# Two convolution projections recast as turns of seven products, with one weight sum of 32 turns made by accumulating transfers

## The chip, the cores and the metric

One core of one Trainium2 chip runs the kernel. The metric is the device time of one execution in microseconds (us); lower is better. The kernel before took 1972.85 us, the median of 3 runs (1972.36 to 1973.45).

## What is computed

One layer on x of 512 tokens by 2048 channels, in float32: a gated short convolution and a squared-ReLU MLP, each behind an RMS norm and with a residual sum. With d = 2048 and an MLP width of 8192 it is, cut to what matters:

```
h = rmsnorm(x, mix_norm)
b_gate, c_gate, v = jnp.split(h @ w_in, 3, axis=-1)      # w_in 2048 x 6144
u = c_gate * v
y = depthwise causal convolution of u over 3 tokens      # conv_w 3 x 2048
x = x + (b_gate * y) @ w_out                             # w_out 2048 x 2048
a = relu(rmsnorm(x, mlp_norm) @ w1)                      # w1 2048 x 8192
x = x + (a * a) @ w2                                     # w2 8192 x 2048
```

## The kernel before, in words

Every product of float32 numbers is made of three matmuls on rounded halves: an operand is split into hi, its rounding to the matmul's format (ScalarE), and lo, the rest (VectorE: operand minus hi), and hi·lo, lo·hi and hi·hi are summed in PSUM.

**Stage one, the convolution** (16 blocks): both projections are made directly. A block is 512 output channels; for each of 16 k-tiles of 128 input channels `products` (L992, matmuls at L989) makes 4 x 3 = 12 matmuls of 128x128 by 128x512, 3072 in all. Weights come in 1 MB loads (L262) into two slots of `w_raw`; `split_hi` (L377, ScalarE) and `split_lo` (L599, VectorE) fill a ring of four. Twelve blocks make c, v and b of four groups of channels; VectorE multiplies and convolves them (`take_c`, `take_v`, `take_b`), the four last blocks are the output projection, whose results are added to x in `resid` (`take_resid`, L666), turned to tokens by 64 transposes of 128x128 (`turn`, L1055) and put to DRAM as `mixed`. The sums of squares for the two norms are made by one matmul (L1012) and eight small ones (L1143).

**Stage two, the MLP** (32 turns): the two products are made by a seven-product (Strassen-Winograd) scheme. A turn `v` takes four quadrants of a weight block (R11, R12, R22, R21, 1 MB each, loaded at L265) and makes the products L11, S1, S2, L12, S3, S4, L22 in this order. Each product has 2 slots, so a turn has 14; a slot is 12 matmuls (L1084), a turn 168. VectorE makes the four weight sums T1 to T4 in place in `raw` (`form_weights`, L793), two instructions of 128x1024 each; T3 is used by S3, slots 8 and 9. Each slot's weights are split by `split_turn_hi` (L454, ScalarE) and `split_turn_lo` (L799, VectorE) into a ring of four, so that the split of slot s waits until TensorE is through with slot s-4. Turns 0 to 15 are the first MLP product ("up"), two turns (a pair) for one group of 1024 hidden channels; 16 to 31 are the second ("down").

In an up pair TensorE waits for two turns' products; ScalarE copies them out of PSUM (L475, L483), VectorE adds them up in 12 steps (`add_up`, L824), ScalarE rectifies, TensorE turns them by 32 transposes (`turn_quad`, L1097, in four groups ahead of slots 0, 2, 4 and 5 of the next pair), ScalarE squares, and the seven activation sums are formed (L679), split (L509, L739) and spilled to DRAM by GpSimd's queue (L351, 14 transfers of 512 KB a pair) to be loaded in the down turns. The activations of the up turns are 7 tiles for either turn of a pair; S2, S4 and L22 have one place for both turns and are reloaded every turn from `act_kept` by the SP queue.

Every engine runs one list of instructions in an order written out by hand: a loop over turns and slots, with tables such as `SPLIT_AT` that say at which slot of which turn a step is made. SP's queue issues the loads in order, each behind a wait; GpSimd's queue issues the stores.

The core of a slot on TensorE:

```
pe.wait_ge(lo_ready, SLOTS * v + s + 1)
for k in (2 * half, 2 * half + 1):
    for t in range(2):
        mm = turn_tile(v, j, k, t)
mm.then_inc(used, 1)
```

Of the kernel before, what the change touches and what calls it, by code (L numbers as in the profile page):

```python
# [12 lines left out]
KT = 16  # L13
# [3 lines left out]
GRAN = 4  # L17
NG = KT // GRAN
NRAW = 2
HALF = 256  # L20
ZBUF = 3

SQUARES_AT = {2: (0,), 3: (1,), 4: (2,), 5: (3, 4), 6: (5,), 7: (6, 7), 8: (8, 9),
              9: (10, 11), 10: (12, 13), 11: (14, 15)}
TAKE_AT = (4, 7, 10, 13)
TURN_AT = (8, 10, 12, 14)

OUT_ORDER = (0, 2, 1, 3)
# [9 lines left out]
NPROD = 7  # L38
R11, R12, R22, R21 = range(4)
RAW_OF = (R11, R11, R11, R21, R12, R22, R21)  # L40
# [4 lines left out]
SHARED = (S2, S4, L22)  # L45
# [4 lines left out]
FIRST_SPLIT = {(1, 11): 0, (1, 12): 1, (1, 13): 2, (1, 15): 3, (2, 0): 4, (2, 2): 5, (2, 4): 6}  # L50
FIRST_FORM = {(1, 14): (0, 1), (2, 1): (2,), (2, 3): (3,)}

SECOND = (L11, L12, S1, S3, S2, S4, L22)
SECOND_SPLIT = {(0, 6): 0, (0, 7): 1, (0, 9): 2, (0, 10): 3, (0, 11): 4, (1, 1): 5, (1, 3): 6}
SECOND_FORM = {(0, 8): (0, 1), (0, 10): (2,), (0, 12): (3,)}
# [4 lines left out]
STAGES = 5  # L60
# [4 lines left out]
def conv_mlp_layer(nc, xt, weights, mlp, cols_dram, out, FF):  # L65
# [4 lines left out]
    OUT0 = 3 * NQ  # L70
    NB = OUT0 + NQ
    NC = FF // (2 * BW)
    NP = NQ // 2
    UP = 2 * NC
    NV = UP + NC * NP
    USED = KT * NB
    assert S == BW and DT == KT and NQ == 4 and weights.shape[0] == NG * NB
    assert mlp.shape[0] == 4 * NV and FF // D * 2 == NC

    xt_v = xt.rearrange("(k p) t -> p k t", p=P)  # L80
    out_v = out.rearrange("(j p) f -> p j f", p=P)
    spill = nc.dram_tensor("spill", (NC, NPROD, 2, P, NT, HALF), F32).ap()
    act_kept = nc.dram_tensor("act_kept", (2, NPROD, 2, P, NT, HALF), F32).ap()
# [5 lines left out]
    RESID, H_HI, H_LO, Z_HI, Z_LO, RAW, RING_AT, U_PAD = (base + KB * a for a in (0, 32, 64, 96, 128, 160, 176, 192))  # L89
    TMP = U_PAD + NT * (CW - 1 + S) * 4  # L90
    RSTD = TMP + 4 * KB
    ONES = RSTD + 2 * KB
    EYE = ONES + 512
    COLS = EYE + 512
    NORM = COLS + (2 + CW) * DT * 4

    with ExitStack() as ctx:
# [3 lines left out]
        def sem(name):  # L101
            return ctx.enter_context(nc.semaphore(name))

        resid = at("resid", RESID, [P, DT, S])
        h_hi = at("h_hi", H_HI, [P, DT, S], F32R)
        h_lo = at("h_lo", H_LO, [P, DT, S], F32R)
        z_hi = at("z_hi", Z_HI, [P, KT, S], F32R)
        z_lo = at("z_lo", Z_LO, [P, KT, S], F32R)
        w_raw = at("w_raw", RAW, [P, NRAW, GRAN, BW])
        w_hi = at("w_hi", RING_AT, [P, RING, BW], F32R)  # L110
        w_lo = at("w_lo", RING_AT + 8 * KB, [P, RING, BW], F32R)
        u_pad = at("u_pad", U_PAD, [P, NT, CW - 1 + S])
        tmp = at("tmp", TMP, [P, 2, S])
        rstd_b = at("rstd_b", RSTD, [P, S])
        ones = at("ones", ONES, [P, P])
        eye = at("eye", EYE, [P, P])
        cols = at("cols", COLS, [P, (2 + CW) * DT])
        square, square_sum = tmp[:, 0, :], tmp[:, 1, :]
        var, root = tmp[:, 0, :], tmp[:, 1, :]


        quads1 = at("quads1", H_LO + 24 * KB, [P, 2, NT, HALF])
        quads2 = at("quads2", U_PAD, [P, 2, NT, HALF])
        quad = {"L11": quads1[:, 0], "L21": quads1[:, 1], "L12": quads2[:, 0], "L22": quads2[:, 1]}
        q_s1, q_s2, q_s3, q_s4 = (at(f"sum{n}", RESID + 4 * KB * n, [P, 2, BW]) for n in range(4))

        q_first = at("sum_first", U_PAD, [P, 2, BW])
        q_l22 = at("sum_l22", H_LO + 28 * KB, [P, 2, BW])
        second_s1 = at("second_s1", RESID + 16 * KB, [P, NT, HALF])
        turned_out = [at("turned0", RSTD, [P, BW])] + [at(f"turned{i + 1}", RESID + a * KB, [P, BW])  # L130
                                                        for i, a in enumerate((12, 14, 20, 22))]
        stage = [at(f"stage{i}", a, [P, NT, HALF], F32R)
                 for i, a in enumerate([RESID + (16 + 4 * i) * KB for i in range(4)] + [TMP])]
        acts1 = [at(f"act{j}", H_HI + 8 * KB * j, [P, 2, NT, HALF], F32R) for j in range(NPROD)]
        acts2 = {j: at(f"act2_{j}", Z_LO + 8 * KB * n, [P, 2, NT, HALF], F32R) for n, j in enumerate((L11, S1, L12, S3))}
        raw = at("raw", Z_HI, [P, 4, NT, BW])
        ring = [at("ring0", RAW, [P, 2, 2, BW], F32R), at("ring1", RAW + 8 * KB, [P, 2, 2, BW], F32R),
                at("ring2", RING_AT, [P, 2, 2, BW], F32R), at("ring3", RING_AT + 8 * KB, [P, 2, 2, BW], F32R)]
        var_t, root_t, rstd_t = (at(f"{n}_t", NORM + 32 * i, [P, NT]) for i, n in enumerate(("var", "root", "rstd")))

        x11, x21, x22, x12 = (at(f"x{q}", Z_LO + 8 * KB * n, [P, NP, 2, BW]) for n, q in enumerate(("11", "21", "22", "12")))
        sum_s1 = [at("sum_s1_0", RESID + 4 * KB, [P, 2, BW]), at("sum_s1_1", RESID + 8 * KB, [P, 2, BW])]
        sum_s2 = [at("sum_s2_0", RESID, [P, 2, BW]), at("sum_s2_1", RESID + 12 * KB, [P, 2, BW])]

        pairs = [ctx.enter_context(nc.psum_tensor(f"pair{i}", [P, 2, BW], F32)) for i in range(NT)]
        ps = [pairs[i // 2][:, i % 2, :] for i in range(2 * NT)]

        X_PARTS = [(k, 1) for k in range(GRAN)] + [(k, GRAN) for k in range(GRAN, DT, GRAN)]
        x_in = [sem(f"x_in{k}") for k, _ in X_PARTS]
        cols_in = sem("cols_in")  # L150
        first_in = [sem(f"first_in{k}") for k in range(GRAN)]
        raw_in = [sem(f"raw_in{i}") for i in range(NRAW)]
        w_hi_ready = sem("w_hi_ready")
        w_lo_ready = sem("w_lo_ready")
        w_used = sem("w_used")
        bank_free = sem("bank_free")
        z_ready = sem("z_ready")
        h_hi_ready = sem("h_hi_ready")
        h_lo_ready = sem("h_lo_ready")
        squared = sem("squared")  # L160
        square_added = sem("square_added")
        ones_ready = sem("ones_ready")
        total_ready = sem("total_ready")
        var_ready = sem("var_ready")
        root_ready = sem("root_ready")
        newton = sem("newton")
        conv_step = sem("conv_step")
        u_ready = sem("u_ready")
        pad_ready = sem("pad_ready")
        stored = sem("stored")  # L170

        turned = sem("turned")
        turn_taken = sem("turn_taken")
        turn_out = sem("turn_out")
        mixed_in = {q: sem(f"mixed_in{q}") for q in ("11", "12", "21", "22")}
# [9 lines left out]
        added = sem("added")  # L185
        rectified = sem("rectified")
# [5 lines left out]
        spilled = [sem(f"spilled{i}") for i in range(STAGES)]  # L192
        raw_turn_in = [sem(f"raw_turn_in{i}") for i in range(4)]
        act_in = [sem(f"act_in{j}") for j in range(NPROD)]
        t_formed = sem("t_formed")
        hi_ready = sem("hi_ready")
# [4 lines left out]
        summed = sem("summed")  # L201

        MIX, MLP = 0, DT
        T1, T2, T3, T4 = 1, 2, 3, 4

        def x_landed(eng, k):

            for s, (first, _) in zip(x_in, X_PARTS):
                if first == k:
                    eng.wait_ge(s, 16)  # L210

        def spills_done(eng, c):
            n = 2 * NPROD * (c + 1)
            for i in range(STAGES):
                eng.wait_ge(spilled[i], 16 * ((n + STAGES - 1 - i) // STAGES))
# [4 lines left out]
        def act_place(v, j):  # L220
            return acts2[j] if v < UP and v % 2 and j not in SHARED else acts1[j]

        def read_out(eng, n):

            v, i = n // 5, n % 5
            if v >= UP:
                eng.wait_ge(taken, n - 5 * UP + 1)
# [10 lines left out]
        def _(sp):  # L238
            def load_x(k, n):
                s = x_in[X_PARTS.index((k, n))]  # L240
                sp.dma_start(resid[:, k:k + n, :], xt_v[:, k:k + n, :]).then_inc(s, 16)

            def load_weights(g, slot):
                sp.dma_start(w_raw[:, slot, :, :],
                             weights[bass.ds(g, 1)].rearrange("a p k n -> p (a k) n")).then_inc(raw_in[slot], 16)


            for k in range(GRAN):
                load_x(k, 1)
# [946 lines left out]
```

## Time and profile before

| what | value |
|---|---|
| median of the runs shown | 1972.85 us |
| the profiled execution, its own time | 1973.64 us |
| its span, first to last instruction | 1971.8 us |
| TensorE busy (instructions) | 1958.0 us, 99% (8778) |
| VectorE busy | 1483.0 us, 75% |
| ScalarE busy | 858.2 us, 44% |
| GpSimd busy | 75.4 us, 4% |
| stage one (convolution), TensorE at L989 | to 716 us |
| stage two, 32 turns | 716 us to the end |
| bytes moved | 445.93 MB, mean 226 GB/s |

How to read it: the profile lists instructions by engine and source line, with start and duration. Successive instructions of one engine overlap a little, so the distance from start to start is shorter than a duration; where an engine is the bound, that distance is what counts. The clock row gives TensorE's granted clock in tenths of full speed.

### The profile page before, as it was taken

Reading aid. Unit: us, or ns where it says so; the run is one execution under the profiler, and the core shown is the slowest. Engines: PE = TensorE matmul, PEld = TensorE weight load, DVE = VectorE, ACT = ScalarE, POOL = GpSimd, SP = SyncE. Lnnn points to the kernel's source line nnn. Section 1 sums busy time; section 2 is a strip of 40 time slices with the busy share of each in tenths; the row PEclk is TensorE's granted clock in tenths of the full one; section 3 lists DMA queues with packets and bytes.
Section 4 is the critical chain, followed back from the end, with each engine's and each line's share of the span. In section 5 each row is a group of like instructions: output and inputs, shape, how many; then the busy total and the mean of one; then the engine's idle time right before and its main releaser. Section 6 shows DMA issues by size and latency. Waiting matters only on the chain.

```text
span 1971.8 us, 23073 instructions
## 1 busy us (share of the span) xinstructions
PE 1958.0 (99%) x8778; PEld 1621.5 (82%) x8778; DVE 1483.0 (75%) x1496; ACT 858.2 (44%) x1002; POOL 75.4 (4%) x146
## 2 busy tenths in 40 slices
PE   8999999999999999999999999999999999999999
PEld 7888888888888888888888888888888888888887
DVE  6335354363453669999999999999899889878878
ACT  6222222222223546656657557575444433334332
POOL 0000000000000100101001011010000000000000
PEclk9999999999999999999999999999999999999999
DMA  5332323222223536667687586789988888887783
GB/s 193 107 107 85 107 85 107 87 105 88 104 93 121 192 111 231 270 250 293 253 321 288 216 323 259 280 327 361 364 341 334 347 319 302 321 329 294 278 330 125
DMA packets 98318, 445.93 MB, mean 226 GB/s; under 512 B 10800, under 2 KB 10800, under 8 KB 73776
## 3 DMA queue, kind: packets, MB, share of 16 engines
q1 hardware_dynamic: 78944, 375.42, 50.5%
q0 software_dynamic: 19136, 69.21, 8.7%
q8 instruction: 58, 0.95, 0.2%
q14 instruction: 36, 0.29, 0.0%
q10 hardware_dynamic: 144, 0.04, 0.0%
HBM read 371.24 MB, written 73.40 MB: 225 GB/s over the span
## 4 chain that ended last, share of the span: by engine, by line
PE 98%; DVE 1%; issue 0%; ACT 0%; DMA 0%; DVEq 0%; ACTq 0%
PE pair L1084 61%; PE pair L989 35%; PE pair L1097 1%; PE pair L1055 0%; DVE raw L793 0%; DVE ring L799 0%; DMA cols<-in_cols 0%; ACT ring L454 0%; DVE act L713 0%; ACT quads L400 0%; PE pair L1019 0%; DVE tmp L614 0%; PE pair L1025 0%; PE pair L1022 0%; ACT L381 0%
## 5 line engine op out<-in xcount | busy, mean ns | idle before, releaser
L1084 PE MATMUL pair<-ring,act 128*128 128x512 f32 x5376 | 1229.3, 390 | 0.1
L1084 PEld LDWEIGHTS pair<-ring,act 128*128 128x128 f32 x5376 | 1006.5, 188 | 208.7 <-DVE ring L799 0.9
L454 ACT ACTIVATE ring<-raw 128x1024 fp32r<-128x1024 f32 x448 | 474.7, 1061 | 565.7 <-PE pair L1084 406.4
L799 DVE TENSOR_TENSOR ring<-raw,ring 128x1024 fp32r<-128x1024 f32 x448 | 537.6, 1219 | 90.0 <-ACT ring L454 89.4
L599 DVE TENSOR_TENSOR w_lo<-w_raw,w_hi 128x512 fp32r<-128x512 f32 x256 | 175.5, 692 | 349.2 <-ACT w_hi L377 343.9
L377 ACT ACTIVATE w_hi<-w_raw 128x512 fp32r<-128x512 f32 x256 | 161.4, 631 | 475.0 <-PE pair L989 471.7
L793 DVE TENSOR_TENSOR raw<-raw 128x1024 f32<-128x1024 f32 x256 | 301.6, 1219 | 5.6
L989 PE MATMUL pair<-h_hi,w_lo 128*128 128x512 f32 x764 | 298.2, 390 | 0.0
L989 PE MATMUL pair<-h_hi,w_hi 128*128 128x512 f32 x764 | 297.5, 389 | 0.0
L989 PE MATMUL pair<-h_lo,w_hi 128*128 128x512 f32 x764 | 297.5, 389 | 0.0
L989 PEld LDWEIGHTS pair<-h_hi,w_lo 128*128 128x128 f32 x764 | 143.6, 188 | 30.6 <-issue 0.8
L989 PEld LDWEIGHTS pair<-h_lo,w_hi 128*128 128x128 f32 x764 | 143.6, 188 | 30.0 <-issue 0.2
L989 PEld LDWEIGHTS pair<-h_hi,w_hi 128*128 128x128 f32 x764 | 143.4, 188 | 29.8
L989 PE MATMUL pair<-z_hi,w_lo 128*128 128x512 f32 x256 | 101.1, 395 | 2.5 <-issue 2.5
L989 PE MATMUL pair<-z_hi,w_hi 128*128 128x512 f32 x256 | 99.9, 390 | 0.0
L989 PE MATMUL pair<-z_lo,w_hi 128*128 128x512 f32 x256 | 99.7, 389 | 0.0
L351 POOL DMA_DIRECT2D spill<-stage x112 | 59.5, 532 | 716.3 <-ACT stage L509 630.5
L739 DVE TENSOR_TENSOR stage<-quads,stage 128x1024 fp32r<-128x1024 f32 x56 | 68.3, 1219 | 10.6 <-ACT stage L509 9.9
L509 ACT ACTIVATE stage<-quads 128x1024 fp32r<-128x1024 f32 x56 | 58.9, 1051 | 8.8 <-DVE quads L679 8.8
L858 DVE TENSOR_TENSOR x<-pair,x 128x1024 f32<-128x1024 f32 x48 | 58.4, 1218 | 1.3 <-PE pair L1084 1.3
L989 PEld LDWEIGHTS pair<-z_hi,w_lo 128*128 128x128 f32 x256 | 48.1, 188 | 12.8 <-issue 3.3
L989 PEld LDWEIGHTS pair<-z_hi,w_hi 128*128 128x128 f32 x256 | 48.1, 188 | 10.3
(89 smaller groups left out, 748.1 us busy)
## 6 DMA issues: line engine op xcount, KB each, us to landing
raw<-in_mlp SPq DMA_DIRECT2D x128, 1024.0 KB, 7.7
act<-spill SPq DMA_DIRECT2D x224, 512.0 KB, 6.5
w_raw<-in_weights SPq DMA_DIRECT2D x63, 1024.0 KB, 4.9
spill<-stage POOLq DMA_DIRECT2D x112, 512.0 KB, 8.4
act<-act_kept SPq DMA_DIRECT2D x84, 512.0 KB, 8.0
act_kept<-act POOLq DMA_DIRECT2D x12, 512.0 KB, 6.3
mixed<-turned POOLq DMA_DIRECT2D x16, 256.0 KB, 2.9
x<-mixed SPq DMA_DIRECT2D x8, 512.0 KB, 12.0
```

What stands on the lines that cost most here:

```text
L351: pool.dma_start(spill[c, SPILLS[n], half], stage[w % STAGES][:].bitcast(F32)).then_inc(spilled[w % STAGES], 16)
L377: nc.scalar.activation(w_hi[:, k % RING, :], w_raw[:, k // GRAN % NRAW, k % GRAN, :], ACT.Copy).then_inc(w_hi_ready, 1)
L454: nc.scalar.activation(ring[g % RING][:, 0], raw[:, r, 2 * (s % 2):2 * (s % 2) + 2, :], ACT.Copy).then_inc(hi_ready, 1)
L509: nc.scalar.activation(stage[w % STAGES][:], quad[HOLDS[SPILLS[n]]], ACT.Copy).then_inc(stage_hi, 1)
L599: nc.vector.tensor_tensor(w_lo[:, k % RING, :], w_raw[:, k // GRAN % NRAW, k % GRAN, :], w_hi[:, k % RING, :].bitcast(F32), ALU.subtract). ...
L739: nc.vector.tensor_tensor(stage[(w + 1) % STAGES][:], quad[HOLDS[SPILLS[n]]], stage[w % STAGES][:].bitcast(F32), ALU.subtract).then_inc(st ...
L793: nc.vector.tensor_tensor(raw[:, o, k:k + 2], raw[:, a, k:k + 2], raw[:, b, k:k + 2], ALU.subtract).then_inc(t_formed, 1)
L799: nc.vector.tensor_tensor(ring[g % RING][:, 1], raw[:, RAW_OF[s // 2], 2 * (s % 2):2 * (s % 2) + 2, :], ring[g % RING][:, 0].bitcast(F32), ...
L858: nc.vector.tensor_tensor(o, bank, o, ALU.add).then_inc(taken, 1)
L989: mm = nc.tensor.matmul(ps[NT * parity + i], stationary, moving, start=(k == 0 and j == 0), stop=(k == KT - 1 and j == 2))
L1084: mm = nc.tensor.matmul(bank, stationary, moving, start=(opens and k == 0 and n == 0), stop=(closes and k == NT - 1 and n == 2))
L1097: tr = nc.tensor.transpose(view[:, i, P * t:P * (t + 1)], o[:, t, P * i:P * (i + 1)], eye[:])
```

## The change

The 16 blocks of the convolution become 16 turns of the same kind as the MLP's, so that the whole kernel is 48 turns: 0 to 11 the input projection (six pairs), 12 to 15 the output projection (two pairs), 16 to 31 up, 32 to 47 down. The kinds of the first 16 pairs are in `KINDS`. A GATED pair gives c and v of a group: VectorE multiplies them while they are in token order (`form_u`), TensorE turns them with 16 transposes ahead of slots 4 and 5 of the next pair, ScalarE takes them out (`take_u`, at its slots 7 and 8) and makes the first tap, VectorE the two others (`more_taps`, 8 instructions of 128x512). A GATE pair gives b: it is scaled, turned with 32 transposes, and VectorE multiplies it into y (`gate`). A MIXED pair gives the output projection; x is added to its sums by accumulating transfers from DRAM (`add_x`), its squares are summed by ScalarE's accumulator.

The norms' sums of squares no longer go through TensorE. x comes in as quadrants, is scaled by ScalarE (`scale_x`), and the seven activation sums of the first two turns are formed and split in place while these turns run (`direct_form`, `direct_hi`, `direct_lo`); so are those of turns 13 and 17. Turns 12 and 16 load theirs from spill. In turns under 16 five activation tiles are shared and reloaded each turn instead of three. The signs of the weight sums are changed so that all four are plain additions, and T3 of the first 32 turns is made by two transfers of GpSimd's queue per turn (512 KB each), which add R22 from DRAM onto R12 in SBUF. They are issued once T1 is formed; ScalarE's splits of slots 8 and 9 wait for them.

```diff
+GATED, GATE, MIXED, UP = range(4)
+KINDS = (GATED, GATED, GATE, GATED, GATED, GATE, MIXED, MIXED) + (UP,) * 8
...
+DIRECT_TURN = {0: 0, 1: 1, V_OUT + 1: 2, V_UP + 1: 3}
...
+DIRECT_SPLIT = {(0, 0): (0, 1), (0, 2): (0, 2), (0, 3): (0, 3), (0, 4): (0, 4), (0, 5): (0, 5), (0, 6): (0, 6),
+                (0, 9): (1, 0), (0, 10): (1, 1), (0, 11): (1, 2), (0, 12): (1, 3), (0, 13): (1, 4), (1, 1): (1, 5),
+                (1, 3): (1, 6)}
+DIRECT_FORM = {(0, 1): (0, 1), (0, 2): (0, 2), (0, 3): (0, 3),
+               (0, 9): (1, 0), (0, 10): (1, 1), (0, 11): (1, 2), (0, 12): (1, 3)}
...
+            load_x(quad["L11"], 0, 0, x_in["L11"])
+            load_raw(0, R11)
+            load_x(quad["L21"], 0, 1, x_in["L21"])
+            load_x(quad["L22"], DT // 2, 1, x_in["L22"])
+            load_raw(0, R12)
+            load_raw(0, R22)
...
+            def add_t3(v):
+
+                pool.wait_ge(t_formed, formed(v, T1))
+                for half in range(2):
+                    k = slice(2 * half, 2 * half + 2)
+                    pool.dma_start(raw[:, R12, k], turns[4 * v + R22, :, k], accum_op=ALU.add).then_inc(t3_in[half], 16)
...
+            for v in range(V_DOWN):
+                q = v // 2
+                stores = v % 2 == 0 and q - 1 in (MIX0, MIX0 + 1)
+                if stores:
+                    for m in range(3):
+                        put_mixed(q - 1, m)
+                add_t3(v)
...
+                elif j == S3 and v < V_DOWN:
+                    act.wait_ge(t3_in[s % 2], 16 * (v + 1))
...
+            scale_x("L11")
+            direct_hi(0, L11)
             for v in range(NV):
+                q = v // 2
                 for s in range(SLOTS):
                     split_turn_hi(v, s)
                     if v == 0:
+                        if s == 0:
+                            scale_x("L21")
+                            scale_x("L22")
+                        if s == 2:
+                            scale_x("L12")
+                        if s in (7, 8):
+                            scale_later(s - 7)
...
                 for k in (0, 2):
                     nc.vector.tensor_tensor(raw[:, o, k:k + 2], raw[:, a, k:k + 2], raw[:, b, k:k + 2],
-                                            ALU.subtract).then_inc(t_formed, 1)
+                                            ALU.add).then_inc(t_formed, 1)
...
+                        if KINDS[q - 1] == GATED:
+                            if s in (2, 3):
+                                form_u(q - 1, s - 2)
+                            if s in (10, 11, 12, 13):
+                                more_taps(q - 1, s - 10)
+                        if KINDS[q - 1] == GATE and s in (3, 5, 6, 7):
+                            gate(q - 1, {3: 0, 5: 1, 6: 2, 7: 3}[s])
...
-                    if s == 5:
+                    if s == 5 and v >= V_DOWN:
                         form_weights(v, T3)
...
+                        if 2 <= v <= V_DOWN and v % 2 == 0:
+                            at_slot = {4: 0, 5: 1} if KINDS[v // 2 - 1] == GATED else {0: 0, 2: 1, 4: 2, 5: 3}
+                            if s in at_slot:
+                                turn_quad(v // 2 - 1, at_slot[s])
```

## Rows read from the trace of the kernel before

**Rows 1.** The page: busy time of TensorE, and its granted clock in 40 slices.

```profile
PE 1958.0 (99%) x8778; PEld 1621.5 (82%) x8778; DVE 1483.0 (75%) x1496; ACT 858.2 (44%) x1002; POOL 75.4 (4%) x146
PEclk9999999999999999999999999999999999999999
```

**Rows 2.** The chain that ended last: start, length, what.

```profile
6.71 2.05 PE pair L1019 x4
...
12.18 30.16 PE pair L989 x132
42.33 0.86 PE pair L1012 x2
...
622.12 1.25 issue
...
669.10 1.25 issue
...
767.64 0.79 PE pair L1143 x8
...
955.54 0.88 PE pair L1097 x8
...
972.73 62.60 PE pair L1084 x276
...
1371.66 595.74 PE pair L1084 x2628
...
1967.43 1.23 DVE x L858
```

**Rows 3.** Busy time by stretch: start of run, one up pair, two down turns.

```profile
10.00:15.00 5.00, 5.00 (x19) 3.96 (x18) 3.59 (x6) 3.40 (x6) 0.00 (x0) 1.00 1.04 411
...
955.54:1035.33 79.79, 79.79 (x370) 66.40 (x369) 76.93 (x68) 49.85 (x54) 7.44 (x14) 1.00 0.71 277
1371.70:1451.50 79.80, 79.80 (x353) 66.08 (x352) 69.97 (x62) 35.38 (x34) 3.19 (x6) 1.00 0.87 334
```

**Rows 4.** Groups of instructions by line, whole run: count, busy, mean ns.

```profile
L799 DVE TENSOR_TENSOR ring<-raw,ring 128x1024 fp32r<-128x1024 f32 x448 | 537.6, 1219 | 90.0 <-ACT ring L454 89.4
...
L793 DVE TENSOR_TENSOR raw<-raw 128x1024 f32<-128x1024 f32 x256 | 301.6, 1219 | 5.6
...
L659 DVE SCALAR_TENSOR_TENSOR tmp<-u_pad,cols,tmp 128x512 f32<-128x512 f32 x32 | 24.0, 751 | 4.7 <-DVE tmp L657 0.2 <-DVE tmp L659 0.2
```

**Rows 5.** VectorE in order of time, in the up pair from 955.54 us.

```profile
954.63 1.22 DVE L793 TENSOR_TENSOR raw<-raw 128x1024 f32<-128x1024 f32 x1
...
956.90 2.35 DVE L799 TENSOR_TENSOR ring<-raw,ring 128x1024 fp32r<-128x1024 f32 x2
959.17 1.22 DVE L824 TENSOR_TENSOR sum_l<-pair,sum_l 128x1024 f32<-128x1024 f32 x1
...
994.33 2.36 DVE L793 TENSOR_TENSOR raw<-raw 128x1024 f32<-128x1024 f32 x2
```

**Rows 6.** ScalarE in order of time, in the same pair.

```profile
973.76 1.07 ACT L454 ACTIVATE ring<-raw 128x1024 fp32r<-128x1024 f32 x1
974.71 1.07 ACT L509 ACTIVATE stage<-quads 128x1024 fp32r<-128x1024 f32 x1
...
1010.95 1.06 ACT L454 ACTIVATE ring<-raw 128x1024 fp32r<-128x1024 f32 x1 [1.66 <-PE pair L1084]
```

**Rows 7.** ScalarE in order of time, start of the run.

```profile
4.04 1.28 ACT L381 ACT_TABLE_LOAD   x1 [4.04 <-DMA cols<-in_cols]
5.33 0.72 ACT L381 ACTIVATE h_hi<-resid,cols 128x512 fp32r<-128x512 f32 x1
5.96 0.61 ACT L377 ACTIVATE w_hi<-w_raw 128x512 fp32r<-128x512 f32 x1
```

**Rows 8.** The spill transfers of L351 (512 KB each, GpSimd's queue).

```profile
DMA to landing us min/median/max: 2.9/8.4/14.2
```

**Rows 9.** The loads of `mixed`, L275 (512 KB each, SP's queue).

```profile
DMA to landing us min/median/max: 7.0/12.0/15.1
```

More of the change, by code:

```diff
@@ L12 @@
 EPS = 1e-6
-KT = 16
 BW = 512
@@ L47 @@
+DIRECT_OF = {Z1: 2, MIX0 + 1: 3}
+SET_PAIRS = [Z0, MIX0] + list(range(UP0, NQP))
+SPILL_SET = {q: n for n, q in enumerate(SET_PAIRS)}
+DIRECT_TURN = {0: 0, 1: 1, V_OUT + 1: 2, V_UP + 1: 3}
 SPILLS = (L11, L22, L12, S1, S3, S2, S4)
 FORMED = {3: 1, 4: 2, 5: 3, 6: 4}
[L50 to L54, printed above, removed]
@@ L66, in conv_mlp_layer, with loaded, loads @@
+def loaded(v):
+    if v >= V_DOWN or v in (V_OUT, V_UP):
+        return PRODUCTS
+    return () if v in DIRECT_TURN else shared(v)
+def loads(v, j):
+    return sum(j in loaded(w) for w in range(v + 1))
+KEPT = (5, 5, 5, 3)
+NORM_X, NORM_M = 6, 14
+def conv_mlp_layer(nc, xt, x, turns, cols_dram, out, FF):
     D, S = xt.shape
@@ L125, in conv_mlp_layer @@
[L125 to L139, printed above, removed]
@@ new lines, in conv_mlp_layer @@
+        later = {"L11": later1[:, 0], "L21": later1[:, 1], "L12": later2[:, 0], "L22": later2[:, 1]}
+        ones = at("ones", MISC, [P, P])
+        eye = at("eye", MISC + 512, [P, P])
+        cols = at("cols", MISC + 1024, [P, (2 + CW) * DT])
+        junk = at("junk", MISC + 1344, [P, BW])
+        NORM = MISC + 1344 + 2 * KB
+        part, part2 = at("part", NORM, [P, NT]), at("part2", NORM + 32, [P, 4, NT])
+        var_t, root_t, rstd_x, rstd_sq, rstd_m = (at(n, NORM + 96 + 32 * i, [P, NT]) for i, n in enumerate(
+            ("var_t", "root_t", "rstd_x", "rstd_sq", "rstd_m")))
@@ L320, in _ @@
                         load_raw(after, r)
-                    if after == UP and j in (L11, S1, L12, S3):
+                    if v == 0 and r == R11:
+                        sp.wait_ge(act_lo_ready, NPROD)
+                        for t in (0, 1):
+                            load_tokens(t)
+                    if after == V_DOWN and j in (L11, S1, L12, S3):
                         product_done(sp, v, j)
@@ new lines, in scale_later, with square_tokens @@
+            def scale_later(n):
+                act.wait_ge(later_in[n], 32)
+                for i in range(NT):
+                    k = MIX + NT + n * DT // 2 + i
+                    o = (later1, later2)[n][:, :, i, :]
+                    nc.scalar.activation(o, o, ACT.Copy, scale=cols[:, k:k + 1]).then_inc(x_scaled, 1)
+            def square_tokens(t):
+                act.wait_ge(x_tok_in[t], 16)
+                nc.scalar.activation(x_tok[t][:], x_tok[t][:], ACT.Square, accum_out=part[:, t:t + 1]).then_inc(squared, 1)
@@ new lines, in take_mixed @@
+            def take_mixed(q, m):
+                act.wait_ge(quad_turned, TURNS[q] + m + 1)
+                quads_free(act, q)
+                f = (0, 1, 1, 0)[m]
+                for i in range(NT):
+                    tile = MLP + NT * (q - MIX0 + 2 * f) + i
+                    ins = nc.scalar.activation(quad[("L11", "L22", "L12", "L21")[m]][:, i, :], by_channels()[:, i, :],
+                                               ACT.Copy, scale=cols[:, tile:tile + 1])
+                ins.then_inc(quad_ready, 1)
@@ new lines, in form_u @@
+            def form_u(q, half):
+                first, s1, _, _, s4, l22 = sums_of(q)
+                o, other = ((first, s4), (l22, s1))[half]
+                dve.wait_ge(added, 12 * q + (11, 12)[half])
+                dve.wait_ge(norm_step, NORM_X)
+                for i in range(2):
+                    nc.vector.scalar_tensor_tensor(out=o[:, i, :], in0=o[:, i, :],
+                                                   scalar=rstd_sq[:, 2 * half + i:2 * half + i + 1], in1=other[:, i, :],
+                                                   op0=ALU.mult, op1=ALU.mult).then_inc(u_formed, 1)
```

1101 lines of the change are left out of this document (451 added, 650 removed).

## Prediction

> **What bounds the kernel now.** I read the page first: TensorE is busy for 1958 of 1971.8 us and its granted clock is full in all slices [rows 1]. Busy time alone proves little, since pipelined matmuls overlap, so the chain of waits comes next. It is TensorE from 6.71 us to 1967.4 us: line 1084 runs 2628 matmuls in one piece of 595.74 us, 0.2267 us each, and the up stage has pieces of 276 in 62.60 us, the same rate [rows 2]. What comes between are transposes and two blocks' ends of 1.25 us [rows 2]. So the time is the number of matmuls times 0.2267 us, plus transposes, plus both ends, as long as the other engines deliver. Then the stretches: an up pair takes 79.79 us with VectorE busy for 76.93 [rows 3]. Its instructions start 1.135 us apart where they follow each other (956.90 to 959.17 for two) though each lasts 1.219 [rows 4, 5]; its 67 instructions so need 76.0 us of 79.79. VectorE is the second bound, 5% away.
>
> **The change, part by part.**
>
> *Matmuls.* Stage one had 16 x 16 x 12 = 3072. Sixteen turns have 16 x 168 = 2688. That is 384 fewer: -87.0 us at 0.2267 [rows 2].
>
> *Transposes.* An up pair has 336 matmuls, 76.17 us, and 32 transposes in the rest of 79.79 us [rows 3]: 0.113 us each. Before: 64 + 8 x 32 = 320. After: 4 gated pairs x 16, 2 gate and 2 mixed x 32, 8 up x 32 = 448. +128 cost +14.5 us.
>
> [...] The rows here say 227 and 113 ns, so I keep those.
>
> *Small TensorE work.* The norm's matmuls (0.86 and 0.79 us) and the two block ends (2 x 1.25 us) go [rows 2]: -4.15 us.
>
> *The start.* Before, matmuls begin at 6.71 us and the first 12 take 5.47 us (to 12.18) for 2.72 [rows 2]. That is 9.5 us lost. After, more must come first. ScalarE is free at about 5.3 us (table load [rows 7]). A 128x512 scale costs 0.63 us from start to start [rows 7], a 128x1024 split 0.95 [rows 6]; a 128x256 scale I estimate at 0.45, on that line. L11: four scales to 7.2, hi 8.25, lo of L11 9.4, lo of slot 0 10.5. TensorE begins at 10.6. Slot 1 needs S1 = L21 - L22: eight scales (12.8), the difference (14.0), its hi (15.0) and lo, then the weight split of slot 1: 17.3. T1 is done at 19.6. From there VectorE is the bound. Turn 0 has 14 splits, 6 sums, 12 activation splits and 8 activation sums, 40 instructions; 7 lie before 19.6, and 32 more end with the split of slot 13: 36.3 us at 1.135 [rows 5]. ScalarE adds some 2.2 us, since it must scale the later x (8 x 0.63) just ahead of the splits of slots 8 to 10. Slot 13's weights are there at 58.1. The split of slot 4 of turn 1 comes 12 instructions later, 71.7. From there TensorE needs 10 slots x 2.72 = 27.2 us and VectorE no longer limits. The first pair ends at 98.9 us, 22.7 more than its 76.2 of matmuls. The loss grows by 13.3 us. The loads hide: weights R12 are the first 3.5 MB in the queue, and the run before moves 411 GB/s at its start [rows 3], so they land by 13 us and are used at 17.3. Without that cover each late us costs one.
>
> *VectorE in the later turns.* T3 leaves: 2 instructions, 2.3 us, a turn. An up pair has 63 instead of 67: 71.5 of 79.8 us. A gated pair has 28 splits, 12 sums and 12 additions, 59.0 us, and leaves 4 products and 8 taps of 0.75 us [rows 4] to the next, 9.0: 68 of 78.0 us (76.17 + 16 x 0.113). The fullest single turns are turn 12 (14 + 6 + 4 + 4 gate + 9 direct = 37, 42.0 us against 41.7 of TensorE) and turn 6 (36). The ring's lead of three slots covers 0.3 us. Cost zero, but for order: in turn 6 `gate` sits on VectorE behind T1, three additions and splits, where before ScalarE squared. By my count of that queue, the group of transposes ahead of slot 4 comes 0.8 us late, and similar meetings in turn 14 (`take_mixed` of 4 short instructions instead of one) and after the gated pairs (TensorE's second group waits for `take_u` at ScalarE's slot 7, 0.5 us in hand) may take a few tenths each. I take 2 us for all.
>
> *T3 by transfers.* They need no engine but GpSimd's queue, which has room (4% busy [rows 1]); there they stand ahead of the turn's spills and behind up to three `mixed` stores, whose sums are ready before T1. What waits is ScalarE, at the split of slot 8, with all its later steps queued behind, then VectorE, then TensorE. In the up pair shown T1 ends at 955.85 and 996.69 [rows 5], and the split of slot 8, by count, starts at 973.76 and 1010.95 [rows 6]: 17.9 and 14.3 us in hand. TensorE comes to slot 8 of the odd turn at 972.73 + 17 x 2.72 = 1019.0 and needs split and rest (2.3 us) first, so it is hit from 20.0 us on, or 19 after the second of two issues. No row shows an accumulating transfer. The nearest are 512 KB transfers of this queue, 2.9 / 8.4 / 14.2 us [rows 8], and at most 15.1 on the other [rows 9]. An accumulate reads its target too, so my ends are 2.9 us and twice 15.1 = 30 us. I take twice the median, 17 us: some waits on ScalarE, none on TensorE. The bytes fit: 1 MB more per 40 us is 26 GB/s on 277 (twice that if the target counts), while the down turns run gapless at 334 [rows 3].
>
> *Other queues.* SP loads 5 tiles instead of 3 in turns 2 to 11, each with 13 slots (35 us) to land; gapless cover by the 334 GB/s above. Turn 16's loads wait for spills of turn 15 slot 3, which at 14.2 us land near slot 8, before SP would issue the next R11 anyway. Zero.
>
> **The sum.** In pieces: first pair 98.9; 46 turns x 168 x 0.2267 = 1751.9; 448 x 0.113 = 50.6; meetings 2; after the last matmul 1971.8 - 1967.4 = 4.4; outside the span 1.84 (1973.64 - 1971.8). That is 1909.7. By differences: 1973.6 - 87.0 + 14.5 - 4.2 + 13.3 + 2 = 1912.2. The two differ by small losses of stage one that only the first leaves out. The profiled execution is 0.8 us above the median, so about 1910 for the median: 3.2% faster. About 0.2% (4 us) is what a measurement can tell from no change.
>
> **The rivals.**
>
> *A, small stalls in many turns* (ScalarE or VectorE order, or T3 at 19 to 21 us): 0.5 to 1 us in each of 46 turns, +23 to +46: 1933 to 1956. For it: VectorE at 95% before had no room tested in this order. Against: T3's 2.3 us a turn leave VectorE.
>
> *B, late sums, slower than before.* T3's transfers land after T1 by more than TensorE can cover. All 32 turns pay. The gain is 63 us, so it is gone at 2.0 us a turn, at a landing of about 21 us; at 24 us it is +5 x 32 = 160: 2070. For it: the end of 30 us. Against: two medians fit.
>
> [...]
>
> [...]
>
> *D, less is saved than the count says*: the direct steps or loads of the start overlap better than my ledger (a pair lost of 12 instead of 22.7 us): 1899.
>
> **How the numbers follow.** Main case (1900 to 1918) 0.68, A 0.12, B 0.07, C 0.05, D 0.08. The prediction is 1910. The low end 1899 is D's; upward the range goes through the lower half of A and of C to 1940. Faster by over 0.2%: all but B and its edge, 0.92. Within: 0.01. Slower: 0.07.
>
> **What would show it.** The chain should stay on the matmul line of the turns from about 75 us to the end, up pairs at 79.8 us, gated successors near 78.0. The first pair should end near 99 us with waits on VectorE. T3's transfers should land under 19 us, with VectorE near 72 of 80 us in up pairs. Wrong would be: waits of ScalarE on the accumulating transfers long enough to show as gaps of TensorE at slot 8, up pairs over 80.5 us, or a matmul spacing other than 0.2267 us.

## The result and the profile after

| kernel | median us | runs | span of the profiled execution |
|---|---|---|---|
| before | 1972.97 | 20 | 1971.8 |
| after | 1976.37 (1973.79 to 1979.58) | 20 | 1975.0 |

The ratio is 1.0018, with a 95% interval of 1.0012 to 1.0024 (here and below, a ratio of the runs can differ by 0.1% from the quotient of the medians): the two are nearly equal, where the prediction said 3.2% faster. 63 of the 66 us between 1910 and 1976 are the expected gain; it did not come. The profiled execution of after took 1976.86 us. Its page has the TensorE row and the clock row that answer to [rows 1]; the busy rows of the 40 slices are left out.

```profile
span 1975.0 us, 22414 instructions
PE 1940.1 (98%) x8512; PEld 1561.9 (79%) x8512; DVE 1710.8 (87%) x1506; ACT 1023.4 (52%) x1102; POOL 168.3 (9%) x262
...
PEclk9999999999999999999999999999999999999999
...
L970 PE MATMUL pair<-ring,act 128*128 128x512 f32 x8064 | 1904.0, 397 | 28.4 <-DVE ring L745 18.6
```

The count is right (8064 + 448 = 8512, 266 fewer than before) and TensorE is as full as before within 1%. It idles for 28.4 us in front of its matmuls, 18.6 of them behind VectorE's splits. So the same span is filled by fewer instructions: look at the rate. In the chain of waits (start, length, what) the lines that answer to [rows 2] are these:

```profile
930.59 0.88 PE pair L990 x8
931.47 5.59 PE pair L970 x24
...
948.07 64.39 PE pair L970 x276
1012.46 0.87 PE pair L990 x8
...
1357.40 613.21 PE pair L970 x2628
```

613.21 us for 2628 matmuls is 0.2333 us each, where [rows 2] have 0.2267. The pieces of 276 take 64.39 instead of 62.60. The transposes take their 0.87 us for eight as before [rows 2], and nothing waits: the piece of 2628 has no gap. Every matmul costs 6.65 ns more; 8064 of them are 53.6 us. The clock isn't the reason: the stretches below (the first pair, then an up pair and two down turns as in [rows 3]) have the granted clock at 1.00 in both of the last, with 0.2333 us in them.

```profile
core 0: us, PE busy (x) PEld busy (x) DVE busy (x) ACT busy (x) POOL busy (x), PEclk, DMA share, GB/s
12.00:22.00 10.00, 8.36 (x24) 5.97 (x24) 6.93 (x7) 5.83 (x11) 0.64 (x1) 1.00 1.04 385
22.00:30.00 8.00, 5.90 (x24) 4.35 (x24) 7.70 (x8) 3.45 (x5) 3.44 (x6) 1.00 1.07 339
30.00:40.00 10.00, 7.10 (x24) 5.55 (x24) 9.97 (x10) 9.36 (x12) 3.18 (x6) 0.83 1.04 360
...
60.00:70.00 10.00, 9.91 (x36) 7.94 (x37) 9.90 (x9) 8.51 (x10) 3.59 (x7) 0.83 1.00 345
...
931.22:1013.09 81.87, 81.87 (x372) 66.29 (x370) 72.95 (x64) 49.80 (x54) 11.12 (x19) 1.00 0.84 295
1421.63:1500.03 78.40, 78.40 (x337) 62.97 (x336) 69.36 (x61) 32.58 (x31) 3.20 (x6) 1.00 0.86 335
```

The up pair takes 81.87 us instead of 79.79 with VectorE busy for less than before (72.95; 76.93 in [rows 3]).

### The profile page after: what moved, and what is told of

It is laid out like the page before. It is cut to its first block, busy times and chain, and to the rows that moved or that the text cites. A ratio compares the mean times of both kernels' runs of the same rounds, so it can differ in the third digit from the quotient of the medians.

```text
span 1975.0 us, 22414 instructions
## 1 busy us (share of the span) xinstructions
PE 1940.1 (98%) x8512; PEld 1561.9 (79%) x8512; DVE 1710.8 (87%) x1506; ACT 1023.4 (52%) x1102; POOL 168.3 (9%) x262
## 4 chain that ended last, share of the span: by engine, by line
PE 91%; DVE 4%; DMA 2%; issue 1%; ACT 1%; POOL 0%; ACTq 0%; DVEq 0%
PE pair L970 89%; PE pair L990 2%; DVE ring L745 1%; DMA raw<-in_turns 1%; DVE raw L739 1%; DMA act_kept<-act 1%; DVE act L707 1%; ACT ring L514 0%; ACT quads L466 0%; DVE sum L776 0%; DMA quads<-in_xt 0%; DVE sum_l_mix L776 0%; ACT act L499 0%; DVE sum L774 0%; DVE quads L804 0%
## 5 line engine op out<-in xcount | busy, mean ns | idle before, releaser
L970 PE MATMUL pair<-ring,act 128*128 128x512 f32 x8064 | 1904.0, 397 | 28.4 <-DVE ring L745 18.6
L970 PEld LDWEIGHTS pair<-ring,act 128*128 128x128 f32 x8064 | 1511.7, 188 | 397.2 <-issue 25.7
L514 ACT ACTIVATE ring<-raw 128x1024 fp32r<-128x1024 f32 x672 | 710.8, 1060 | 888.8 <-PE pair L970 611.2
L745 DVE TENSOR_TENSOR ring<-raw,ring 128x1024 fp32r<-128x1024 f32 x672 | 810.4, 1221 | 192.9 <-ACT ring L514 191.8
L739 DVE TENSOR_TENSOR raw<-raw 128x1024 f32<-128x1024 f32 x320 | 377.3, 1221 | 8.6 <-DMA raw<-in_turns 0.7
L410 POOL DMA_DIRECT2D raw<-in_turns x64 | 57.0, 1035 | 718.5 <-DVE raw L739 718.5
L613 ACT ACTIVATE stage<-quads 128x1024 fp32r<-128x1024 f32 x70 | 73.4, 1049 | 10.6 <-DVE quads L679 8.9
L776 DVE TENSOR_TENSOR sum<-pair,sum 128x1024 f32<-128x1024 f32 x64 | 78.0, 1218 | 0.0
L540 ACT ACTIVATE sum<-pair 128x1024 f32<-128x1024 f32 x64 | 64.6, 1009 | 0.0
L774 DVE TENSOR_TENSOR sum<-sum,sum 128x1024 f32<-128x1024 f32 x32 | 39.0, 1218 | 0.0
L776 DVE TENSOR_TENSOR sum<-sum,sum 128x1024 f32<-128x1024 f32 x32 | 37.7, 1218 | 0.8 <-issue 0.7
L840 DVE TENSOR_TENSOR sum_s<-pair,sum_s 128x1024 f32<-128x1024 f32 x28 | 34.1, 1218 | 0.0
```

The lines of the kernel that those rows point to most:

```text
L410: pool.dma_start(raw[:, R12, k], turns[4 * v + R22, :, k], accum_op=ALU.add).then_inc(t3_in[half], 16)
L514: nc.scalar.activation(ring[g % RING][:, 0], raw[:, RAW_OF[j], 2 * (s % 2):2 * (s % 2) + 2, :], ACT.Copy).then_inc(hi_ready, 1)
L540: nc.scalar.activation(sums_of(q)[1 + i][:], pairs[2 + (5 * v + i) % 2][:], ACT.Copy).then_inc(copied, 1)
L613: nc.scalar.activation(stage[w % STAGES][:], quad[HOLDS[SPILLS[n]]], ACT.Copy).then_inc(stage_hi, 1)
L739: nc.vector.tensor_tensor(raw[:, o, k:k + 2], raw[:, a, k:k + 2], raw[:, b, k:k + 2], ALU.add).then_inc(t_formed, 1)
L745: nc.vector.tensor_tensor(ring[g % RING][:, 1], raw[:, RAW_OF[s // 2], 2 * (s % 2):2 * (s % 2) + 2, :], ring[g % RING][:, 0].bitcast(F32), ...
```

## The experiments

### What sets the matmul's spacing

Two things differ for a matmul of the turns between the two kernels: what else runs (more DMA bytes, the accumulating transfers), and where its operands lie in SBUF. The layout was in the diff, but not in my prediction. Of the kernel after:

```
base = 16512
ACTS1, ACTS2 = base, base + 56 * KB
RAW = base + 88 * KB + 32
RING_AT, SUMS, QUADS, STAGE = RAW + 32 * KB, RAW + 64 * KB, RAW + 80 * KB, RAW + 96 * KB
```

`u_pad`, the last tile before `RAW`, is 4 x 514 x 4 = 8224 bytes long, so `RAW` is moved by 32 bytes over a whole number of KB. The ring lies behind `RAW` and moves with it; the activations don't. In the turns the activations are the stationary operand and the ring is the moving one. Before, all of these tiles lay at whole KB from each other. The theory is that the place of the ring relative to the activations costs the 6.65 ns; the rival is that the traffic does. The expectations call the first theory P (place), in this form: the moving operand starts 32 bytes off a multiple of 64, that start costs the 6.65 ns, and a start at a multiple of 64 gives 0.2267 us again. The rival is theory D there.

**Align 64.** The kernel after with one number changed.

```diff
-    RAW = base + 88 * KB + 32
+    RAW = base + 88 * KB + 64
```

> Edit: in the changed kernel the weight tiles and all that lies behind them (raw, ring, sums, quads, stage) start 64 bytes past a multiple of 64 instead of 32, nothing else. [...] It expects 0.2267 us again, up pairs of 79.8 us for 81.9, and 7700 x 6.65 ns = 51 us less: about 1925 us, ratio 0.976. Theory D (transfers): the higher traffic (300 for 226 GB/s) or the 64 accumulating transfers slow TensorE's reads: spacing stays at 0.2333, time 1976. Theory C (clock, mean 0.996 for 1.000): stays too.

Measured: 1947.38 us against 1973.3, a ratio of 0.9872 (0.9856 to 0.9889). The spacing in the piece of 2628 is 601.54 / 2628 = 0.2289 us. 32 bytes took 29 us off. So the place matters, but a multiple of 64 isn't enough.

**The kernel before, shifted by 32 bytes.** The same offset put into the kernel that had none, without anything else of the change.

```diff
+    RAW, RING_AT, U_PAD = RAW + 32, RING_AT + 32, U_PAD + 32
```

> Edit: in the kernel before, the raw and ring tiles and what lies behind them are moved by 32 bytes, nothing else. In stage one these tiles are the stationary operand, in the turns the moving one. Theory P expects the turns at 0.2333 us a matmul, 5376 x 6.65 ns = +35.7 us, up pairs of 82.0 us, and stage one unchanged at 0.227 us if only the moving operand counts: 2008.6 us, ratio 1.018. If the stationary operand counts too, stage one grows as well, by up to 20 us. Theories D and C expect no change, 1973 us, since no transfer changes.

Measured: 2025.78 us, a ratio of 1.0266 (1.0249 to 1.0283), 52.5 us slower. Its chain:

```profile
43.86 574.00 PE pair L990 x2460
...
1161.24 64.39 PE pair L1085 x276
...
1406.90 613.21 PE pair L1085 x2628
```

64.39 and 613.21 are to the hundredth the values of the kernel after, with no accumulating transfer and 446 MB of traffic instead of 593. Stage one, where the weights are the stationary operand, has 574.00 / 2460 = 0.2333 as well. This is the decisive run: the place alone makes the whole difference in rate, and traffic makes none.

**The kernel before, shifted by 64 bytes** (the same line with 64; one run).

> Edit: as the run before, but moved by 64 bytes. A control of the shift by 32. Theory P: spacing 0.2267 us, 1973 us. A theory that the distance between ring and activation tiles counts, and not the 64-byte boundary: a change here too.

Measured: 2003.54 us. Turns 0.2289 us, but stage one 0.2333:

```profile
43.88 574.01 PE pair L990 x2460
...
1315.40 63.17 PE pair L1085 x276
1395.83 601.55 PE pair L1085 x2628
```

My first form of the theory, P, fails here: by it both stages would be at 0.2267 us at 64. In stage one moving and stationary operand have changed places, and so has the sign of the distance between them (-64 instead of +64). The distance seemed to be what counts.

**Align 128**, as align 64 with 128.

> Edit: as the run with 64 bytes, but the weight tiles and what lies behind them start 128 bytes on, which puts the ring at a multiple of 128 again, as in the kernel before. The first call showed three levels of spacing in the turns: 0.2267 us (offset 0), 0.2289 (64), 0.2333 (32), in both kernels. Theory P2 (the start of the ring modulo 128 bytes, relative to the activation tiles or absolute) expects 0.2267 us: 7700 x 2.2 ns = 17 us below the run with 64 bytes, about 1930 us, ratio 0.978. Theory P3 (any distance from the old place counts, the larger the boundary the more) expects 0.2289 or above, 1947 us.

Measured: 1967.92 us against 1972.75, 0.9975 (0.9964 to 0.9985), and 610.71 / 2628 = 0.2324 us. More alignment is slower than 64: this rules out every rule of the kind "aligned to at least n bytes" up to 128.

**The kernel before with all tiles moved by 64** (one run).

```diff
-    base = 16512
+    base = 16512 + 64
```

> Edit: in the kernel before, every tile is moved by 64 bytes, so that both operands of every matmul keep their distance and lose their old start modulo 128. Theory P-rel (the distance of the two operands modulo 128 counts) expects 0.2267 us a matmul in both stages, 1973 us. Theory P-abs (each start modulo 128 counts by itself) expects 0.2289 us or more in the turns and up to 0.2333 in stage one, 2003 us or more.

Measured: 1973.74 us, 595.77 us for 2628, 0.2267 us each. Moving everything together by 64 bytes costs nothing; the distance does.

**A distance of 256** in the kernel after (`88 * KB + 256`), and in the kernel before (the line of the shift by 32, with 256; one run).

> Edit: the changed kernel with the weight tiles and what follows 256 bytes on instead of 32. Theory R modulo 256: 0.2267 us, 1925 us. Theory R modulo 512 or 1024: another level between 0.228 and 0.234, 1940 to 1980 us.

> Edit: the kernel before with raw, ring and what follows moved by 256 bytes. The same question in the other kernel, for both stages: modulo 256 gives 0.2267 us in both and 1973 us; otherwise more in one or both, up to 2026 us.

Measured: after 1934.37 us against 1973.4, 0.9801 (0.9788 to 0.9815), with 595.76 us for 2628; before 1972.48 us, with 595.74 us for 2628 and 547.00 for 2412 in stage one. Both are at 0.2267 us. With 0 and 256 alike and 32, 64 and 128 each dearer, a price that goes by the distance modulo 256 bytes fits all the distances tried (in the table, what is left beyond whole KB):

| distance of moving from stationary, bytes | us a matmul | runs that show it |
|---|---|---|
| 0 | 0.2267 | before, base + 64, ring in front (below) |
| +256, -256 | 0.2267 | after + 256; before + 256 (turns; stage one) |
| +32, -32 | 0.2333 | after, before + 32 (turns; stage one) |
| +64 | 0.2289 | align 64, before + 64 (turns) |
| -64 | 0.2333 | before + 64 (stage one) |
| +128 | 0.2324 | align 128 |

+64 was measured in the turns alone and -64 in stage one alone, so whether the sign or the stage makes 0.2333 out of 0.2289 isn't shown.

**The ring in front.** The other way to a distance of whole KB: the ring lies at `base`, the activations behind it, and only `raw`, which no matmul reads, keeps the odd 32 bytes.

```diff
-    ACTS1, ACTS2 = base, base + 56 * KB
-    RAW = base + 88 * KB + 32
-    RING_AT, SUMS, QUADS, STAGE = RAW + 32 * KB, RAW + 64 * KB, RAW + 80 * KB, RAW + 96 * KB
+    RING_AT, ACTS1, ACTS2 = base, base + 32 * KB, base + 88 * KB
+    RAW = base + 120 * KB + 32
+    SUMS, QUADS, STAGE = RAW + 32 * KB, RAW + 48 * KB, RAW + 64 * KB
```

> Edit: the changed kernel with the ring moved ahead of the activation tiles, so that the 32 bytes that u_pad takes over 8 KB no longer lie between them; the distance of ring and activations is a multiple of 1024 bytes, as in the kernel before. Seen so far, by the distance beyond that: 0 gives 0.2267 us a matmul in the turns (also with both moved by 64 bytes), 64 gives 0.2289, 128 gives 0.2324, 32 gives 0.2333. Theory R (the two operands' relative place modulo some power of two up to 1024 bytes sets the spacing) expects 0.2267 us, 7700 x 6.6 ns = 51 us less than the changed kernel, 1925 us, ratio 0.976. A theory that something else of the new layout counts (the absolute places, or which lies lower) expects another level, 1940 us or more.

Measured: 1932.86 us against 1973.4, 0.9805 (0.9791 to 0.9818). It and the distance of 256 are the fastest complete versions of all, 2% under both kernels, and can't be told apart.

```profile
1251.07 62.59 PE pair L970 x276
...
1330.86 595.77 PE pair L970 x2628
1926.65 1.22 DVE x L840
```

Against the kernel after that is 43.5 us. The rate alone is 53.6: some 10 us of it lay under waits, which grew as the matmuls got faster. By the starts of each turn's first matmul, turns 14 and 15 lose 4.8 us more above their matmuls than at the slow rate, the first pair 1.5 us more, and the first turn after each gated pair 0.4.

### T3 by transfers or by VectorE

From align 64, T3 of the first 32 turns is put back on VectorE at slot 5.

```diff
-                add_t3(v)
...
-                elif j == S3 and v < V_DOWN:
-                    act.wait_ge(t3_in[s % 2], 16 * (v + 1))
...
-                    if s == 5 and v >= V_DOWN:
+                    if s == 5:
                         form_weights(v, T3)
```

> Edit: the aligned changed kernel, with T3 of the first 32 turns made by VectorE again at slot 5 and no accumulating transfers of weights. It adds 64 instructions of 1.135 us on VectorE. Theory V (the transfers were worth it, VectorE is the bound wherever it is full): up pairs as before, 79.8 us, since 67 instructions fit; the first pair and the pairs after GATE pairs, where VectorE is the bound, grow by 2.3 us a turn: in all +5 to +25 us on the aligned kernel. Theory D (the transfers cost more than they save): faster than the aligned kernel by up to 20 us.

Measured: 1950.03 us, 0.9883 (0.9867 to 0.9900) of before; align 64 is 0.9872 (0.9856 to 0.9889). The transfers are worth 2.65 us of 1950. The two intervals overlap, and it is less than either theory expected and less than a tenth of the loss. The up pairs take 80.4 us in both. The change's transfers neither hurt nor matter much. Their landing in the kernel after (view of line 410):

```profile
L410 POOL DMA_DIRECT2D raw<-in_turns x64: 853/962/1268, 21.4 to 1300.9; - x64
...
DMA to landing us min/median/max: 6.4/10.0/14.5
```

### What delays turn 16

With the rate explained, after (and each of its copies) has a second loss, where the convolution ends. By the waits of TensorE between 600 and 705 us and of ScalarE between 640 and 705 us in the kernel after (engine, line, waited for, us in total, times, longest):

```profile
PE pair L970 <- DVE sum L776: 6.5, 1, 6.5
PE pair L990 <- ACT quads L593: 1.2, 1, 1.2
```

```profile
ACT ring L514 <- DMA raw<-in_turns: 18.8, 3, 11.7
ACT ring L514 <- DVE raw L739: 10.2, 3, 5.6
```

Two suspects: R11 of turn 16, which SP issues behind its wait for turn 15's spills (issued at 660.6 us, landed about 676.7), and the accumulating transfers of x, for which VectorE's sums of the mixed pairs wait.

**R11 first.** Distance 128 and SP loads R11 of turn 16 ahead of its wait for the spills.

```diff
+                if after == V_UP:
+                    sp.wait_ge(t_formed, formed(v, T4))
+                    load_raw(after, R11)
...
-                        sp.wait_ge(t_formed, formed(v, T4))
-                        load_raw(after, r)
+                        if after != V_UP:
+                            sp.wait_ge(t_formed, formed(v, T4))
+                            load_raw(after, r)
```

> Edit: the 128-byte kernel, and at turn 16 SP issues the load of R11 before it waits for the spills of the first mixed pair. In the changed kernel ScalarE waits 11.7 us for that load there, with 2 MB of activations ahead of it in the queue. Theory Q (the order of this queue is the cause): 8 to 10 us less than the 128-byte kernel, near 1921 us, and the 11.7 us wait gone. Theory B (bandwidth: 12 MB in 40 us are late in any order): less than 3 us, and another tile is late.

Measured: 1972.65 us, ratio 1.0000 (0.9991 to 1.0009), 4.7 us slower than align 128. The longest wait moved and didn't shrink:

```profile
ACT ring L518 <- DVE raw L743: 20.3, 4, 14.0
...
ACT ring L518 <- DMA raw<-in_turns: 4.2, 1, 4.2
```

```profile
PE pair L974 <- DVE sum L780: 9.3, 1, 9.3
```

ScalarE's longest wait for a weight load falls from 12.2 us in align 128 to 4.2, but it waits 14.0 us for a weight sum of VectorE, and TensorE 9.3 us for the sums instead of 6.9 in align 128. R11 was one of several transfers in a stretch where the DMA share is full (from 640 to 700 us it is 1.05 in the kernel after, and 0.79 from 180 to 270). That bringing one forward holds others back fits the x transfers, the longest of which landed after 25.3 us instead of 20.8 in align 128, but no run singles it out.

**R11 first, and one semaphore for each kept tile.** In turn 1 every shared activation waits for all ten `act_kept` stores of turn 0; here each waits for its own two.

```diff
-                        act.wait_ge(act_out, 16 * 2 * KEPT[0])
+                        act.wait_ge(kept0[j], 32)
```

> Edit: as the run before, and the split of each shared activation tile of turn 1 waits for the store of its own tile of turn 0 alone, not for those of all five. In the changed kernel ScalarE waits 3.5 us for the stores of the five, in a stretch where VectorE is the bound. Theory K expects the start of the chain's steady part 2 to 3.5 us earlier and the time by as much less, about 1918 us. If the first pair is held by VectorE's count alone: no change.

Measured: 1972.2 us, ratio 0.9995 (0.9986 to 1.0004), 0.4 us off the run before it, which the intervals don't separate. In the kernel after, ScalarE waited once for `act_kept`, 3.5 us. At distance 128 that wait is in neither profile, and the first pair lasts 92.0 us from its first matmul in both. So this pair says only that the semaphore is free; it doesn't price the wait (with it, the pair lasts 94.3 us in the kernel after).

**Ring in front, without x.** The eight accumulating transfers and VectorE's waits for them are gone. The output lacks x in the convolution's residual sum.

```diff
-                    pool.wait_ge(copied, 5 * q + 4)
-                    add_x(q, "12", s4)
...
-                    pool.wait_ge(added, 12 * q + 4)
-                    add_x(q, "22", s1)
+                    pass
-                if KINDS[q] == MIXED and n in (4, 6, 9, 10):
-                    dve.wait_ge(x_added[{4: "12", 6: "11", 9: "22", 10: "21"}[n]], 16 * (q - MIX0 + 1))
```

> Edit: the ring-front kernel without the eight accumulating transfers that add x to the sums of the two mixed pairs (this leaves out the residual x of the convolution's sum). In the changed kernel they take 11 to 21 us to land; VectorE waits 5.2 us for one in turn 15, and TensorE 6.5 us behind it. Theory X (they cost TensorE time at the end of the second mixed pair) expects 6 to 12 us less than the ring-front kernel. If the load of R11 for turn 16 (11.7 us wait) sets the end there all the same: under 3 us.

Measured: 1925.0 us against 1932.86 with them, 7.9 us less (ratio to before 0.9758, 0.9743 to 0.9773). Waits of TensorE between 575 and 720 us, first with x and then without:

```profile
PE pair L970 <- DVE sum L776: 7.8, 1, 7.8
PE pair L990 <- ACT quads L593: 2.2, 1, 2.2
```

```profile
PE pair L981 <- ACT quads L586: 2.0, 1, 2.0
PE pair L961 <- issue: 0.3, 1, 0.3
```

The wait of 7.8 us in turn 15 is gone. So is one of 2.2 us ahead of turn 14 (the second line with x), before which VectorE waited 2.0 us for one of these transfers; the 2.0 us without x is another wait, in turn 16. By the starts of the first matmuls, turns 13 to 15 take 12.5 us less and turn 16 takes 3.8 us more. So 7.9 us is a net price, and that it comes so near the wait of 7.8 is luck. Whether the landing of the x transfers costs it, or the room that they take in the queues, isn't separated.

A part of it is TensorE's clock. Around each of these waits the granted clock is 0.50 for a few us (6.7 with x, 3.3 without). With x:

```profile
666.46 7.76 PE L970 MATMUL pair<-ring,act 128*128 128x512 f32 x24 [7.82 <-DVE sum L776]
```

```profile
664.00:670.70 6.70, 4.24 (x10) 3.40 (x11) 4.33 (x5) 2.00 (x2) 0.00 (x0) 0.50 1.02 424
```

Without x:

```profile
671.40:674.70 3.30, 3.30 (x11) 2.62 (x10) 3.30 (x3) 1.08 (x2) 1.30 (x2) 0.50 1.03 428
```

The 24 matmuls behind the wait take 7.76 us, where 24 of them take 5.71 in turn 6 of the same kernel: 2 us more. In the kernel before, the clock is 1.00 from 640 to 700 us.

The x transfers land later than any other of their queue, where the medians of the other lines are 8.3 to 10.0 us and the longest landing is 18.2 (line 416 of the kernel after):

```profile
L416 POOL DMA_DIRECT2D sum<-in_x x4: 1192/1226/1272, 560.3 to 662.8; - x4
...
DMA to landing us min/median/max: 11.2/14.5/20.9
```

## Why the prediction was wrong

**The step that failed** is the first of its ledger, "384 fewer: -87.0 us at 0.2267", and with it "46 turns x 168 x 0.2267 = 1751.9". It took the spacing of before as a constant of this kind of matmul, and priced 8064 matmuls of a new layout with it. They took 0.2333. The prediction did name this as what would make it wrong ("a matmul spacing other than 0.2267 us"), but gave it no chance: rival C, at 0.05, was a low rate of TensorE in the first pair only. The count and the transposes' price held. The layout lines stood in the diff, and the odd 32 in them had no counterpart before. The rows of before couldn't price it, since every matmul there runs at distance 0; but an unpriced change is to be bounded, not left out.

Of 66 us, the rate took 43.5 (after against ring in front). The other 23 are seen best in ring in front, where the rate is the predicted one. The starts of the first matmuls of the turns give the loss of each above 168 x 0.2267:

| part | predicted | ring in front |
|---|---|---|
| first pair, to the first matmul of turn 2 | 98.9 us | 105.3 |
| turns 2 to 13 beyond transposes | in the 2 for meetings | 4.4 |
| turns 14 and 15 beyond transposes | in the 2 for meetings | 13.0 |
| turns 16 and 17 beyond transposes | 0 | 1.1 |
| turns 18 to 47 beyond transposes | 0 | 0 |

That is 6.4 + 18.5 - 2 = 22.9 us, the gap from 1910 to 1932.9.

- *The first pair* was to lose 22.7 us and loses 29.1 (30.3 in the kernel after, where it ends at 106.5). The steps of the ledger hold to a few us in the kernel after: T1 done at 21.0 (19.6), slot 13 at 62.4 (58.1), slot 4 of turn 1 at about 77 (71.7). What it left out: ScalarE's table load waits for x to land (5.55 instead of 4.04 us in [rows 7]); ScalarE waits 3.5 us for the `act_kept` stores; and the granted clock is 0.50 from 34.3 to 37.6 and from 61.6 to 64.9 us, which makes the 0.83 of the two stretches shown above. Rival C foresaw a low rate as a state of the whole pair, up to 1964 us. No run shows that term, which is also behind the upper end of the range; what the kernel after shows is these two stretches of 3.3 us and the first 12 matmuls, which take 5.30 us, and the next 12 3.06, though the granted clock reads 1.00 there too. The latter costs nothing, as the next weights are ready at 18.6 us only. The clock explains little of the loss: with R11 first (distance 128) it is 1.00 from 11 to 103 us and the wait for `act_kept` is missing, and still the pair lasts 92.0 us from its first matmul, where 98.9 - 10.6 = 88.3 were predicted. With a stretch at 0.51 (34.1 to 37.5 us), R11 first with its own semaphores takes the same 92.0. What is left, some 3 us, is steps ahead of slot 4 of turn 1 that take longer than counted; no run takes them apart. In the kernel after, the chain there begins as follows.

```profile
0.81 4.67 DMA quads<-in_xt
5.55 1.28 ACT L466
6.84 1.71 ACT quads L466 x4
...
39.45 14.68 DMA act_kept<-act
```

- *Meetings.* Turn 6 came about as counted (0.8): TensorE waits 0.7 us for VectorE's `gate` at the transposes ahead of slot 4 in the kernel after, and 1.2 us in ring in front. Turns 2 to 13 lose 4.4 us instead of under 2, of which turns 2 and 6 lose 1.4 and 1.5. What was missed is in turns 14 and 15: the change said that x is added by accumulating transfers, and the ledger gave them no line. They cost 7.9 us, shown by leaving them out.
- *Turn 16's loads*, "zero": in the kernel after the spills are in at 658.8 us, which is near slot 8 of turn 15 (658.0) as counted. But T4 of that turn is formed at 656.0, so the spills do hold R11 back. It is issued at 660.6, behind four transfers of activations, and lands at 676.7: 16.1 us, where the loads of this kind take 7.6 in the median of the run. While the x transfers are there, loading R11 first didn't help. Without them 5.7 us remain in turns 13 to 17, 4.3 of them in turn 16, and there the chain that ended last goes through a spill and R11's load:

```profile
631.63 15.32 DMA spill<-stage
...
648.87 10.84 DMA raw<-in_turns
...
668.91 1.56 ACT quads L586 x4
...
670.61 1.27 PE pair L981 x8
671.88 6.89 PE pair L961 x24
```

  ScalarE waits 8.1 us for that load, TensorE then 2.0 us for ScalarE, and the transposes and matmuls behind take 1.7 us more, with the granted clock at 0.50 from 671.4 to 674.7 us. So the trace puts most of the 4.3 us behind a step that the prediction had at zero. No run loads R11 first without the x transfers, so what that would give back isn't shown.
- *T3 by transfers*, priced at zero with a landing of 17 us: right. Median 10.0, longest 14.5 us, under the 19 that TensorE can cover. Rival B needed 21 us and fell by that. Twice the median was my estimate, on the ground that the target is read too; no run shows that ground, and the factor was too high: an accumulating transfer of weights took 1.2 times the median of [rows 8] (10.0 against 8.4). The issues of line 410 take 0.85 to 1.27 us beside a VectorE that is busy for 73 of 82 us, so none is held up long.
- *Rival A*, small stalls in many turns: no. The up and down turns of ring in front have none, an up pair takes 79.79 us as in [rows 3], and 62.59 us is the piece of 276.
- *Rival D*, a shorter first pair: no, it was longer.
- *The rates.* The rows' values were the right kind: 226.7 to 233.3 ns a matmul and 109 a transpose (0.87 us for eight).

## What to carry to other kernels

When a change moves tiles, compare the distance between the two operands of every hot matmul before and after: a spacing from a trace is the price of that layout too, and 32 odd bytes ahead of one operand cost 2.7% of a kernel that TensorE bounds (before + 32: 2025.78 us). Keep the distance at a multiple of 256 bytes (whole KB and 256 beyond are what was measured, both at 0.2267 us); 224 more bytes of padding gave back 2.1% here. When the predicted gain is missing and nothing waits, divide the longest gapless piece of the chain by its count first.

## What the hardware showed that was not expected

- The spacing of float32r matmuls of 128x128 by 128x512 at full clock depends on the distance of moving from stationary operand in SBUF: 0.2267 us at 0 and 256 bytes, 0.2289 at +64, 0.2324 at +128, 0.2333 at +32, -32 and -64. All tiles moved by 64 together: 0.2267. What in the chip makes it so isn't shown by these runs; my first form of the theory (a start at a multiple of 64 bytes is free) was refuted by before + 64, and other distances weren't tried. -64 is from the stage in which the two operands have changed places.
- Accumulating transfers of 512 KB from DRAM onto SBUF landed in 6.4 / 10.0 / 14.5 us (least, median, most, 64 of them, weights) and 11.2 / 14.5 / 20.9 us (8 of them, x), beside plain stores of the same size and queue in 2.9 / 9.6 / 18.2 us.
- The granted clock fell to 0.50 around single waits of TensorE in an otherwise full run: in ring in front it waits from 658.6 to 666.5 us, the clock is at 0.50 from 664.0 to 670.7, and the 24 matmuls behind the wait take 7.76 instead of 5.71 us. Without the x transfers, TensorE waits 2.0 us, to 670.6, and the clock is at 0.50 from 671.4 to 674.7.
